# A two-layer encoder trunk on one core: VectorE writes a weight block's rest one step later, behind that step's bank emptyings, in the gate and up steps from the twentieth on

## The reference

```python
h = rms_norm(x, norm_ffn_g[l])
x = x + (jax.nn.silu(h @ w_gate[l]) * (h @ w_up[l])) @ w_down[l]
```

## Time and profile before

| | |
|---|---|
| median of 3 executions | 2075.53 us (2075.39 to 2075.8) |
| the profiled execution, its own time | 2075.76 us |
| span from its first to its last instruction | 2073.9 us |
| TensorE matmul busy | 2051.7 us, 99% |
| VectorE busy | 1423.6 us, 69% |
| ScalarE busy | 829.7 us, 40% |
| granted TensorE clock, mean | 0.998 |

### The profile page before, as it was taken

One profiled execution on the slowest core, in us unless ns is written; L12 is line 12 of the kernel. 1 busy time (PEld: TensorE's weight loads), 2 busy tenths in 40 slices (PEclk: granted clock), 3 DMA queues, 4 the chain that ended last, 5 costly groups with the idle time before them and its releaser, 6 DMA issues.

```text
span 2073.9 us, 27799 instructions
## 1 busy us (share of the span) xinstructions
PE 2051.7 (99%) x10316; PEld 1696.2 (82%) x10316; DVE 1423.6 (69%) x2320; ACT 829.7 (40%) x1466; POOL 228.6 (11%) x135
## 2 busy tenths in 40 slices
PE   8999999999999999999999999999999999999998
PEld 7888778888888888888898887788788888888887
DVE  6323773789877778787833338647998777777877
ACT  4221683453333333444612227734433333344443
POOL 1331034300000000000033301341000000000000
PEclk9999999999999999999999999999999999999999
DMA  5222433224333236633221314441243323383333
GB/s 182 72 92 61 143 122 124 81 72 170 131 105 114 93 114 252 198 97 97 77 81 61 102 41 145 142 149 49 82 173 127 107 97 109 110 306 120 97 97 122
DMA packets 111061, 244.40 MB, mean 118 GB/s; under 512 B 13649, under 2 KB 18641, under 8 KB 110673
## 3 DMA queue, kind: packets, MB, share of 16 engines
q1 hardware_dynamic: 97056, 214.32, 31.7%
q10 hardware_dynamic: 13872, 28.31, 3.7%
HBM read 191.73 MB, written 50.86 MB: 117 GB/s over the span
## 4 chain that ended last, share of the span: by engine, by line
PE 92%; DVE 5%; issue 1%; ACT 1%; DMA 1%; POOL 0%; ACTq 0%; DVEq 0%; POOLq 0%
PE bank L1811 28%; PE bank L1813 27%; PE bank L1812 27%; PE bank L1990 2%; PE bank L1971 2%; PE bank L1955 2%; DVE s_lo L1197 1%; DVE t_lo L1477 0%; PE bank L2012 0%; DMA w_g<-in_wg 0%; PE bank L1905 0%; PE bank L1934 0%; PE bank L2005 0%; DVE hid_cu L1590 0%; PE bank L2030 0%
## 5 line engine op out<-in xcount | busy, mean ns | idle before, releaser
L1811 PE MATMUL bank<-t_hi,s_hi 128*128 128x512 f32 (+1 forms) x1336 | 517.3, 387 | 3.2 <-DVE hid_cu L1590 1.4
L1812 PE MATMUL bank<-t_lo,s_hi 128*128 128x512 f32 (+1 forms) x1336 | 516.4, 386 | 0.0
L1813 PE MATMUL bank<-t_hi,s_lo 128*128 128x512 f32 (+1 forms) x1336 | 516.3, 386 | 0.0
L1811 PEld LDWEIGHTS bank<-t_hi,s_hi 128*128 128x128 f32 x1336 | 250.9, 188 | 56.3 <-DVE hid_cu L1590 2.3
L1813 PEld LDWEIGHTS bank<-t_hi,s_lo 128*128 128x128 f32 x1336 | 250.9, 188 | 50.9
L1812 PEld LDWEIGHTS bank<-t_lo,s_hi 128*128 128x128 f32 x1336 | 250.9, 188 | 50.6
L663 POOL TENSOR_TENSOR w_lo<-w_raw,w_hi 128x1024 fp32r<-128x1024 f32 x65 | 161.7, 2499 | 944.0 <-ACT w_hi L749 802.5
L1811 PE MATMUL bank<-b_hi,s_hi 128*128 128x512 f32 x528 | 206.0, 390 | 0.1
L1813 PE MATMUL bank<-b_hi,s_lo 128*128 128x512 f32 x528 | 205.5, 389 | 0.0
L1812 PE MATMUL bank<-b_lo,s_hi 128*128 128x512 f32 x528 | 205.4, 389 | 0.0
L1811 PE MATMUL bank<-h_hi,w_hi 128*128 128x512 f32 x512 | 201.0, 393 | 0.0
(11 more groups left out here) (218 smaller groups left out, 3195.5 us busy)
## 6 DMA issues: line engine op xcount, KB each, us to landing
w_g<-in_wg SPq DMA_DIRECT2D x44, 512.0 KB, 3.5
w_u<-in_wu SPq DMA_DIRECT2D x44, 512.0 KB, 4.4
t_raw<-hidden_t SPq DMA_DIRECT2D x88, 256.0 KB, 2.6
bias<-in_bias SPq DMA_DIRECT2D x24, 768.0 KB, 5.6
w_raw<-in_win SPq DMA_DIRECT2D x34, 512.0 KB, 3.8
t_raw<-hidden_b SPq DMA_DIRECT2D x66, 256.0 KB, 2.6
hidden_b<-hid_g SPq DMA_DIRECT2D x60, 256.0 KB, 2.0
hidden_t<-hid_x SPq DMA_DIRECT2D x44, 256.0 KB, 2.0
```

The costliest lines, as they stand in the source:

```text
L1811: nc.tensor.matmul(bank, lh, rh, start=start, stop=False)
L1812: nc.tensor.matmul(bank, lh, rl, start=False, stop=False)
L1813: return nc.tensor.matmul(bank, ll, rh, start=False, stop=stop)
```

## The change

In turns `s` above 19 the rest that VectorE writes is that of step `s + 3` in place of `s + 4`, and it stands behind `gate_up(s)`, and behind a late sum where there is one, but ahead of the other sums. Turn 19 writes no rest, so that none is written twice; one more call behind the loop writes the last one. Turns up to 18 stay as they were.

```diff
                     late = [AT_STEP[p, j] for p in range(1, FRONT) for j in (4, 5)]
                     if s + LEAD in late:
                         ring_sum(l, s + LEAD)
+                    if s > 19:
+                        prepare_lo(l, s + LEAD - 1)
                     if s + LEAD + 1 not in late:
                         ring_sum(l, s + LEAD + 1)
-                    prepare_lo(l, s + LEAD)
+                    if s < 19:
+                        prepare_lo(l, s + LEAD)
                     if s in (1, 8):
                         mixed_operand({1: 2, 8: 3}[s])
                     if s in (12, 16, 18):
                         last_operands({12: 4, 16: 5, 18: 6}[s])
                 gate_up(GU_STEPS)
+                prepare_lo(l, GU_STEPS + LEAD - 1)
                 for r in range(DN_STEPS):
```

## The result

| | us, median (lowest to highest) |
|---|---|
| before, in the comparison | 2075.53 (2075.32 to 2075.99), 5 runs |
| after | 2084.89 (2084.78 to 2086.74), 5 runs |
| ratio | 1.0047, 95% interval 1.0032 to 1.0062 |
| profiled execution of after | own time 2085.63, span 2083.8 |

The change makes the kernel 9.4 us, or 0.47%, slower. The forecast was 2084.8.

What follows compares the result with a forecast made beforehand. TensorE, busy 99% of the span, was taken as the bound. Losses of 3.6 + 0.6 + 0.5 us in layer 0 and 3.5 + 0.6 + 0.5 in layer 1, +9.3, gave a median of 2084.8 us, range 2080.5 to 2092.5.

Steps and rivals of the forecast that it cites:

- What bounds it, and what the edit does: Whole kernel: TensorE busy 99% of the span; pairs 4 to 10 lose nothing, covered by VectorE's 23% to spare.
- The rest of step 25 and the load of `w_u1`: Layer 0, pair 1: rest held behind the `w_g1` sum; step 25 0.43 us late, `w_u1` issued at 473.39 instead of 469.13.
- The trips: Loads of `w_u1` in pairs 1 to 3: travelling alone, each takes 3.6 us, against 4.5 beside `w_g1`.
- The upper bound of the sum: Both layers, with longer `w_u1` trips: +7.4 us in layer 0 and +9.8 in layer 1, 17.2 in all.
- Steps 27 to 30: Layer 0, first stretch: turns of 3.36, 3.24, 3.36 us against 2.72 a step; 3.6 us lost for the stretch.
- Layer 1: First stretch, with `w_g1` taking 5.2 us: step 25 2.1 us late, step 27 2.6 late, 3.5 us in all.
- Pairs 2 and 3: Later pairs with late sums, each layer: 0.6 us lost in pair 2 and 0.5 in pair 3.
- Faster: Rival: banks emptied sooner, rests still in time; at most 3.6 us won, giving 2071.9; chance 0.04.
- No change: Rival: three steps of lead absorb the late rests; within 4 us, about 2077; chance 0.11.
- The clock: Rival: waits of 2 us at step 26 drop TensorE to 1.2 GHz; add 5, 2090; chance 0.05, shared with longer trips.

Runs made afterwards that it cites:

- the order alone from pair 4 on: The changed kernel with its new order only in turns above 55, so in pairs 4 to 10; 2075.84 us, ratio to before 0.9998.
- a `w_u1` of 1.65 us: The changed kernel, loads of `w_u1` for pairs 1 to 3 cut to 64 of 1024 columns (32 KB); 2078.33 us, ratio 1.0011.
- the late sums together: The kernel before, with both late sums of pair 1 moved behind turn 23's emptyings and the rest of step 26 following; 2072.99 us, ratio 0.9985.
- turns 22, 32 and 42 mended: The changed kernel, but in turns 22, 32 and 42 the rest stands ahead of the late sum on `w_g1`; 2077.37 us, ratio 1.0008.
- loads in series: The kernel before, but SyncE waits for `w_g1` to land before issuing `w_u1` in pairs 1 to 3; 2075.89 us, ratio 0.9999.
- pairs 1 to 3 only: The changed kernel with its new order only in turns 20 to 56; 2086.57 us, ratio to before 1.0048.
- the rest ahead of the late sum: The changed kernel, but in the six turns with a late sum the rest stands ahead of that sum; 2076.57 us, ratio to before 1.0003.
- turns 23, 33, 43 mended: The changed kernel, but in turns 23, 33 and 43 the rest stands ahead of the late sum on `w_u1`; 2080.89 us, ratio 1.0026.
- the second profile of after: Profile from measuring the changed kernel again, with nothing altered; 2084.73 us, ratio to before 1.0044.

## Why the prediction was right

**What bounds it, and what the edit does.** TensorE sets the end, and VectorE's order costs only where TensorE waits; from pair 4 on nothing was to be lost. Right: 267.00 of 267 us busy, and the order alone from pair 4 on changed nothing.

**The rest of step 25 and the load of `w_u1`.** Forecast for layer 0: `w_g` sum waits 2.2 us, `w_u` sum 1.7, issues 4.9 apart, step 25 0.43 late, step 26 with 2 us of wait. Measured 2.12, 1.57, 4.74, 0.36 and 1.88. That this is the cause, and not the lost overlap or the shorter lead, was argued in the prediction and is shown by the runs: the one rest put back ahead of the one sum (turns 22, 32, 42) takes away 7.4 of the 8.8 us.

**The trips.** 3.6 us for a `w_u1` that travels alone: 3.47, the median of after's loads. The term enters six times. The estimate of 3.2 us from the Trainium skill, page "DMA: Bandwidth & Descriptors", section "Anatomy of one DMA — SWDGE (gpsimd) path", is 0.3 too low here; the sum by it, about +7, and the rows' +9.3 lie on the two sides of the 8.7 that the profile gives to the change. The upper bound of the sum does not follow from its terms: with `w_u1` at 5.2 us in layer 1, its own terms (3.5 + 1.6 and 1.5 for each of pairs 2 and 3) give 8.1 there and not 9.8, so 15.5 in all and not 17.2. The measured time is far below either.

**Steps 27 to 30.** The turns were 3.48, 3.43 and 3.26 us from rest to rest, where 3.36, 3.24 and 3.36 were forecast. In the first two the sum behind the rest started 0.82 behind it (478.66 to 479.48), and I had 0.72; in the third it started 0.60 behind. These errors nearly cancel, and layer 0's first stretch comes to 3.5 net (4.4 less 0.9), against 3.6.

**Layer 1.** This term rested on a trip of 5.2 us for `w_g1`, which was one execution's. It was 3.4 in after's, so the sum there waited 2.10 us and not 3.9, and step 25 was 0.36 us late and not 2.1. The chain of waits was right there too, but its size was not: I had layer 1 at 4.6, and it was 3.4. Layer 0 I had at 4.7, and it was 5.3. That the total of +9.3 comes so near (8.7 in the profile, 9.4 between medians) is in part luck: one layer was too high and the other too low.

**Pairs 2 and 3.** Forecast 1.1 us in each layer. Measured 1.6 in layer 0 and 1.3 in layer 1, at steps 38, 39 and 49.

**The rivals.** *Faster* needed trips of 3.1 and 1.5 us; with a `w_u1` of 1.65 us the kernel was still 2.4 us slower than before. But the rival was right in what there was to win: 3.6 us at most, and the kernel with the late sums together won 3.2. *No change* needed rests that do not hold the load. The run with turns 22, 32 and 42 mended is that case, and it came to 2077.37, about the 2077 given for it. *The clock* did fall in after's layer 1 behind such a wait, and that cost at most 0.3 us (below).

## What to carry to other kernels

In a queue that is worked off in order, look first at what stands behind an instruction that waits for a load: if the issue of the next load hangs on it, one wait becomes two trips one behind the other. A shorter lead or a lost overlap of loads, which come with it, can cost little or nothing (here 1.2 us in a layer, and nothing), so try each by itself. Put behind the issue, and ahead of the waiting instruction, work that others wait for and that needs no load.

## What the runs showed of the hardware

**A load that meets a fetch of instructions.** Before's trip of 5.2 us has a neighbour that the one of 3.5 in layer 0 has not. The DMA queues in the 8 us around before's loads in layer 1 (packets, MB, share of 16 engines):
```profile
q1 hardware_dynamic: 288, 1.05, 37.0%
q8 instruction: 1, 0.02, 1.1%
```
Layer 0's window has the same 288 packets of q1 and no q8. In this place (pair 1 of layer 1) a `w_g1` took 5.2, 5.4, 4.9 and 4.7 us in four profiles (before, and the kernels from pair 4 on, with loads in series and with the late sums together), each with one such packet 1.2 to 2.7 us behind its issue; in the eight others it took 3.4 to 3.7 and had none. A `w_u1` that met one without `w_g1` doing so took 5.0 and 4.4 us (turns 22, 32, 42 mended; pairs 1 to 3 only). But 4.4 us also came without one, for a `w_u1` that overlapped `w_g1` (the rest ahead of the late sum), and in pair 2 nine loads of `w_g1` met a packet 2.9 us or more behind their issue and took 3.3 to 3.8. So the packet must fall early on the load, if it is the cause. It is a coincidence, not tried by itself.

**A trip against its size.** The loads of 32, 256 and 512 KB that SyncE issues alone took 1.65, 2.36 and 3.5 us, about 1.5 us and 3.9 ns for each KB (some 265 GB/s) by the smallest and the largest; the middle one was 0.2 us faster than that line. The Trainium skill, page "DMA: Bandwidth & Descriptors", section "Anatomy of one DMA — SWDGE (gpsimd) path", gives an estimate of 2.1, 2.6 and 3.2 for a copy that GpSimd issues: its fixed part is longer and its bytes are faster than what these runs show for SyncE's. No run here shows such a load issued by GpSimd.

**The clock behind a wait.** In layer 1 of after, TensorE waited 1.86 us at step 26, and then went on like this:
```profile
1508.44 0.47 PE L1815 MATMUL bank<-t_hi,s_hi 128*128 128x512 f32 x1 [1.86 <-DVE s_lo L1197]
...
1510.33 0.63 PE L1816 MATMUL bank<-t_lo,s_hi 128*128 128x512 f32 x1
1510.76 0.63 PE L1817 MATMUL bank<-t_hi,s_lo 128*128 128x512 f32 x1
...
1513.31 0.40 PE L1817 MATMUL bank<-t_hi,s_lo 128*128 128x512 f32 x1
1513.55 0.40 PE L1815 MATMUL bank<-t_hi,s_hi 128*128 128x512 f32 x1
```
```profile
1487.00:1514.00 27.00, 24.65 (x99) 19.18 (x98) 22.43 (x37) 9.66 (x17) 0.00 (x0) 0.94 0.24 78
```
Eight matmuls are 0.43 apart in place of 0.227, the level of 1.2 GHz, with a granted clock of 0.94 over the stretch, which the page's row doesn't show. The same came in layer 1 of the kernel with pairs 1 to 3 only, behind 2.74 us. Eight waits of 1.6 to 2.7 us stand in four profiles (the two of after, pairs 1 to 3 only, turns 23, 33, 43 mended), and the low level came behind two of them. It did not come in layer 0 behind 1.88 us, nor in either layer of the second profile of after (1.90 and 1.79 us lost at step 26, clock 1.00 throughout); there layer 1 cost 3.1 us over before, and with the low level 3.4. The eight matmuls were 1.6 us slower, and by that comparison not more than 0.3 us of it counted: in the second profile TensorE lost 1.2 us at steps 27 and 28 to their rests, at the full clock. Why the clock fell behind one wait and not behind the other stays open. The Trainium skill, page "TensorE: Matmul & The Clock Gate", section "Why this matters for your kernels", warns of idle gaps between bursts that are longer than these. The trace shows the fall behind 1.86 and 2.74 us as well, so the gap need not be that long; and where another engine set the pace, it cost at most 0.3 of 1.6 us.
